# State-space heads and attention heads of a two-block mixer in one interleaved order, with the spreading products on all 128 rows

## What is computed

```python
def ssd_chunked(x, dt, A, Bm, Cm):
    a_cum = jnp.cumsum(a, axis=-1)
    seg = jnp.exp(jnp.where(causal, a_cum[..., :, None] - a_cum[..., None, :], -jnp.inf))
    cb = jnp.einsum('bclhn,bcshn->bhcls', Cm, Bm)
    y_diag = jnp.einsum('bhcls,bcshp->bclhp', cb * seg, xdt)      # 8 state-space heads of 64
...
def fox_mixer(q, k, v, f_raw, f_b):                                # 4 attention heads with a forget gate
    c = jnp.cumsum(log_f, axis=1).transpose(0, 2, 1)
    s = jnp.einsum('bqhd,bkhd->bhqk', q[:, q0:q1], k[:, :q1]).astype(jnp.float32) * scale
    return s + (c[:, :, q0:q1, None] - c[:, :, None, :q1])
...
def mla_mixer(...):                                                # 4 attention heads
        s = jnp.einsum('bqhd,bkhd->bhqk', q_nope[:, q0:q1], k_nope[:, :q1])
        s = s + jnp.einsum('bqhr,bkr->bhqk', q_rope[:, q0:q1], k_rope[:, :q1])
...
    mix = jnp.concatenate([y_ssd, y_fox.astype(h.dtype), y_mla.astype(h.dtype)], axis=-1) @ w_out[l]
```

## Time and profile before

| | before |
|---|---|
| median of 3 runs | 2350.14 us |
| the profiled execution | 2333.99 us |
| its span | 2331.9 us |
| TensorE busy | 2142.1 us (92%) |
| VectorE busy | 1222.7 us (52%) |
| ScalarE busy | 875.1 us (38%) |
| GpSimd busy | 709.2 us (30%) |
| mean granted clock of TensorE | 0.942 |

### The profile page before, as it was taken

One profiled execution on the slowest core, in us unless ns is written; L12 is line 12 of the kernel. 1 busy time (PEld: TensorE's weight loads), 2 busy tenths in 40 slices (PEclk: granted clock), 3 DMA queues, 4 the chain that ended last, 5 costly groups with the idle time before them and its releaser, 6 DMA issues.

```text
span 2331.9 us, 40609 instructions
## 1 busy us (share of the span) xinstructions
PE 2142.1 (92%) x17634; PEld 1918.1 (82%) x17634; DVE 1222.7 (52%) x2199; ACT 875.1 (38%) x1262; POOL 709.2 (30%) x316
## 2 busy tenths in 40 slices
PE   4989988999889989999999898899999998889997
PEld 3867866889887868898999785699989997758897
DVE  6155445763672447653652665565265419437652
ACT  0442111444443223544433444243343335334443
POOL 0340001314672003126315550131551175204124
PEclk9998997999998989999999997899999998869999
DMA  8563441455343003554454340244444543203552
GB/s 327 229 258 146 147 161 61 155 187 185 141 157 115 2 2 128 193 185 163 163 181 165 128 160 1 91 164 180 170 142 177 179 165 116 102 16 139 189 185 87
DMA packets 49681, 340.43 MB, mean 146 GB/s; under 512 B 6368, under 2 KB 8416, under 8 KB 8672
## 3 DMA queue, kind: packets, MB, share of 16 engines
q1 hardware_dynamic: 49504, 337.84, 40.2%
HBM read 336.77 MB, written 1.05 MB: 145 GB/s over the span
## 4 chain that ended last, share of the span: by engine, by line
PE 82%; DVE 11%; ACT 2%; issue 2%; DMA 2%; POOL 1%; SPq 0%; ACTq 0%; DVEq 0%; POOLq 0%
PE bank L529 81%; DMA ada_ring<-ada 2%; POOL ring_low L2442 1%; PE bank L535 1%; DVE arena L1842 1%; DVE small L1837 1%; DVE arena L1827 1%; ACT high L1429 1%; DVE arena L1870 1%; DVE arena_parts L1865 1%; DVE ZZ L2049 0%; DVE arena L1857 0%; DVE ada_ring L2350 0%; DVE arena L2393 0%; DVE small L2300 0%
## 5 line engine op out<-in xcount | busy, mean ns | idle before, releaser
L529 PE MATMUL bank<-arena_parts,high 128*128 128x272 f32 (+2 forms) x4512 | 1023.9, 315 | 60.0 <-ACT arena_parts L1454 38.0
L529 PEld LDWEIGHTS bank<-arena_parts,high 128*128 128x128 f32 x4512 | 748.0, 191 | 110.0 <-issue 48.7
L529 PE MATMUL bank<-arena_parts,ring_low 128*128 128x272 f32 (+2 forms) x2736 | 781.0, 288 | 0.0
L1429 ACT ACTIVATE high<-ring 128x2048 fp32r<-128x2048 f32 x237 | 453.2, 1914 | 676.9 <-PE bank L529 591.4
L2442 POOL TENSOR_TENSOR ring_low<-ring,high 128x2048 fp32r<-128x2048 f32 x105 | 485.5, 4627 | 721.0 <-ACT high L1429 721.0
L529 PEld LDWEIGHTS bank<-arena_parts,ring_low 128*128 128x128 f32 (+1 forms) x2736 | 522.6, 191 | 1.0
L1878 DVE TENSOR_TENSOR ring_low<-ring,high 128x2048 fp32r<-128x2048 f32 x132 | 303.9, 2302 | 180.6 <-ACT high L1429 180.6
L529 PE MATMUL bank<-hidden_high,high 128*128 128x256 f32 (+1 forms) x1056 | 303.2, 287 | 0.0
L529 PE MATMUL bank<-hidden_low,high 128*128 128x256 f32 (+1 forms) x1056 | 301.1, 285 | 0.0
L529 PE MATMUL bank<-hidden_high,ring_low 128*128 128x256 f32 (+1 forms) x1056 | 300.2, 284 | 0.0
L2442 POOL TENSOR_TENSOR hidden_low<-arena,hidden_high 128x256 fp32r<-128x256 f32 (+1 forms) x132 | 111.9, 850 | 575.1 <-DVE hidden_high L1894 575.1
(11 more groups left out here) (317 smaller groups left out, 2291.8 us busy)
## 6 DMA issues: line engine op xcount, KB each, us to landing
ring<-stream SPq DMA_DIRECT2D x269, 1024.0 KB, 4.8
ada_ring<-ada SPq DMA_DIRECT2D x48, 1024.0 KB, 6.0
con<-consts SPq DMA_DIRECT2D x1, 1542.5 KB, 11.3
con<-consts SPq DMA_DIRECT2D x1, 1040.0 KB, 7.0
arena<-xin SPq DMA_DIRECT2D x1, 1024.0 KB, 11.5
out<-arena SPq DMA_DIRECT2D x2, 512.0 KB, 2.9
prob_even<-consts SPq DMA_DIRECT2D x1, 320.0 KB, 11.6
par<-params SPq DMA_DIRECT2D x1, 272.5 KB, 9.3
```

The lines of the kernel that those rows point to most:

```text
L529: ins = nc.tensor.matmul(o, l, r, start=start, stop=stop_, skip_group_check=True)
L1429: act(high[:, q % HIGHS], ring[:, s % RING], ACT.Copy).then_inc(a.sig(high_ready), 1)
```

## The change

**Rows.** The running sums and the forget-gate products take all 128 rows of `sel12` and of `arena[:, 9, 5]` and `arena[:, 9, 6]` instead of 12. The added rows of `sel12` are zeros already; for the added rows of the tiles, VectorE clears `arena[:, 9, 5:7]` at the start of `mixer(l)`.

**Order.** TensorE does running sums 0 to 3, logits 0, running sums 4 and 5, state-space product 0, running sums 6 and 7, state-space product 1, logits 1, state-space products 2 and 3, and then the transposes. VectorE and ScalarE follow in an order that fits. The norm's sums by `ones` move behind logits 2, its root behind the last exponentials, and its reciprocal to the end of VectorE's part.

**Memory and semaphores.** The running sums use banks 6, 7, 4 and 5 instead of 0 to 3, so that logits 0 has banks 0 to 3. `prob(2)` and `prob(3)` move from slot 6 to the memory behind `EE`. ScalarE's decay exponentials get a semaphore of their own, and `sloped` counts every head.

```diff
         def prob(h):
-            return (prob_even, arena[:, 2, 4:7], arena[:, 6, 0:3], arena[:, 6, 3:6])[h % 4]
+            o = 8 * 432 + 3 * TALL * (h % 2)
+            return (prob_even, arena[:, 2, 4:7])[h % 4] if h % 4 < 2 else spare[:, o:o + 3 * TALL].rearrange("p (i t) -> p i t", i=3)
...
-                for h in range(8):
-                    b = h % 4
+                def running_sum(h):
+
+                    b = (6, 7, 4, 5, 4, 5, 4, 5)[h]
                     if h < 4:
                         eng.wait_ge(*freed(b))
-                    elif h % 2 == 0:
-                        eng.wait_ge(sloped, pe.nth(sloped))
-                    mm(bank[b][:, 0:T], cm("sel12", P, P * h, 12), arena[0:12, 9, 5, 0:T], True, True,
+                    else:
+                        eng.wait_ge(sloped, pe.nth(sloped, 3 if h == 4 else 1))
+                    mm(bank[b][:, 0:T], cm("sel12", P, P * h), arena[:, 9, 5, 0:T], True, True,
                        hold=True).then_inc(told(b, "vector"), 1)
...
-                                m = mm(to(e), cm("sel12", qn, P * (8 + h), 12), arena[0:12, 9, 6, 0:kn], False, True, hold=i)
+                                m = mm(to(e), cm("sel12", qn, P * (8 + h)), arena[:, 9, 6, 0:kn], False, True, hold=i)
...
+                for h in range(4):
+                    running_sum(h)
+                for b in range(4):
+                    eng.wait_ge(*freed(b))
                 logits(0)
...
+                running_sum(4)
+                running_sum(5)
+                state_space(0)
+                running_sum(6)
+                running_sum(7)
+                state_space(1)
+                eng.wait_ge(logits_masked, pe.nth(logits_masked, 6))
+                logits(1)
+                state_space(2)
+                state_space(3)
+                eng.wait_ge(sloped, pe.nth(sloped, 2))
                 for p in range(4):
-                    if p == 0:
-                        eng.wait_ge(logits_masked, pe.nth(logits_masked, 6))
-                        logits(1)
                     for e in range(2):
                         turned(2 * p + e)
                     if p < 2:
                         eng.wait_ge(logits_masked, pe.nth(logits_masked, 6))
                         logits(p + 2)
+                    if p == 0:
+                        eng.wait_ge(a2p, pe.nth(a2p))
+                        for g in range(2):
...
                     attended(p)
```

ScalarE, whose whole new order of this part is:

```diff
+                decays(0)
+                decays(1)
                 exps(0)
                 exps(1)
...
+                decays(2)
+                decays(3)
+                exps(2)
+                exps(3)
+                eng.wait_ge(v2a, a.nth(v2a))
+                act(arena[:, 2, 0:4, 0:T], arena[:, US, 0:4, 0:T], ACT.Square).then_inc(a.sig(a2p), 1)
+                turned(0)
+                turned(1)
+                turned(2)
+                exps(4)
+                turned(3)
+                exps(5)
+                attended(0)
+                turned(4)
+                exps(6)
+                turned(5)
+                exps(7)
+                eng.wait_ge(v2a, a.nth(v2a))
+                act(small[:, 0:2, 0:T], small[:, 0:2, 0:T], ACT.Sqrt).then_inc(a.sig(a2v), 1)
+                attended(1)
+                turned(6)
+                turned(7)
                 attended(2)
                 attended(3)
```

VectorE:

```diff
             def mixer(l):
                 eng.wait_ge(*v.last)
+                nv.memset(arena[:, 9, 5:7, :], 0.0).then_inc(v.sig(vstep), 1)
+                eng.wait_ge(*v.last)
...
+                slopes(0)
+                slopes(1)
+                weighted(0)
                 masked(0)
                 masked(1)
+                slopes(2)
+                weighted(1)
+                ssd_out(l, 0)
+                slopes(3)
+                weighted(2)
+                ssd_out(l, 1)
+                masked(2)
+                weighted(3)
+                masked(3)
+                ssd_out(l, 2)
+                ssd_out(l, 3)
+                finish(0)
+                finish(1)
                 for g in range(2):
                     eng.wait_ge(full_for_vector[6 + g], v.nth(full_for_vector[6 + g]))
                     nv.tensor_scalar(small[:, g, 0:T], bank[6 + g][:, 0:T], 1.0 / 256, EPS_LN, ALU.mult, ALU.add).then_inc(v.sig(free["vector"][6 + g]), 1)
...
+                nv.memset(cols[:, 59:60], 0.0).then_inc(v.sig(v2a), 1)
+                for h in range(2, 6):
                     finish(h)
...
+                    masked(h + 2)
+                finish(6)
+                finish(7)
+                eng.wait_ge(a2v, v.nth(a2v))
+                nv.reciprocal(small[:, 0:2, 0:T], small[:, 0:2, 0:T]).then_inc(v.sig(vstep), 1)
```

More of the change, by code:

```diff
@@ L1380, in mixer @@
                         logits(p + 2)
+                    if p == 0:
+                        eng.wait_ge(a2p, pe.nth(a2p))
+                        for g in range(2):
+                            eng.wait_ge(*freed(6 + g))
+                            for k in range(2):
+                                m = mm(bank[6 + g][:, 0:T], cm("ones"), tl(2, 2 * g + k, T), k == 0, k == 1, hold=k)
+                                if k:
+                                    m.then_inc(closing(6 + g, "vector"), 1)
                     attended(p)
@@ L1713, in mixer, with decays @@
                     act(MV[0:sn, i], bank[b][0:sn, 256:512], ACT.Copy).then_inc(a.sig(free["scalar"][b]), 1)
[L1714 to L1718 removed]
+                def decays(j):
+                    eng.wait_ge(sloped, a.nth(sloped, 2))
+                    act(EE[:, 2 * j:2 * j + 2], EE[:, 2 * j:2 * j + 2], ACT.Exp).then_inc(a.sig(decays_ready), 1)
                 def exps(h):
@@ L1737, in attended @@
                     act(tl(US, 4 + p, T), bank[b][:, 0:T], ACT.Copy).then_inc(a.sig(free["scalar"][b]), 1)
+                decays(0)
+                decays(1)
                 exps(0)
                 exps(1)
-                for h in range(8):
-                    if h < 6:
-                        exps(h + 2)
-                    turned(h)
-                    if h == 3:
-                        eng.wait_ge(v2a, a.nth(v2a))
-                        act(small[:, 0:2, 0:T], small[:, 0:2, 0:T], ACT.Sqrt).then_inc(a.sig(a2v), 1)
-                    if h in (3, 5):
-                        attended(h // 2 - 1)
+                decays(2)
[20 more added lines that the diff above has]
+                turned(7)
                 attended(2)
@@ L2350, in slopes @@
                             nv.tensor_scalar(EE[0:sn, h, PK[i]:PK[i] + T - s0], bank[b][0:sn, s0:T], decay_col(i, h, sn), 0.0,
[L2351 removed]
+                                             ALU.add, ALU.min).then_inc(v.sig(sloped if i == 2 else vstep), 1)
                 def weighted(j):
[L2355 removed]
+                    eng.wait_ge(decays_ready, v.nth(decays_ready))
                     x = EE[:, 2 * j:2 * j + 2]
                     nv.tensor_tensor(x, x, CB[:, j // 2].unsqueeze(1).to_broadcast([P, 2, 432]), ALU.mult).then_inc(v.sig(decayed), 1)
[L2359 to L2372 removed]
                 def masked(h):
@@ L2399, in mixer @@
                     nv.tensor_scalar(small[:, g, 0:T], bank[6 + g][:, 0:T], 1.0 / 256, EPS_LN, ALU.mult, ALU.add).then_inc(v.sig(free["vector"][6 + g]), 1)
-                for h in range(8):
-                    if h < 6:
-                        masked(h + 2)
-                    if h == 3:
-                        nv.memset(cols[:, 59:60], 0.0).then_inc(v.sig(v2a), 1)
-                    finish(h)
-                    if h == 5:
-                        eng.wait_ge(a2v, v.nth(a2v))
-                        nv.reciprocal(small[:, 0:2, 0:T], small[:, 0:2, 0:T]).then_inc(v.sig(vstep), 1)
+                nv.memset(cols[:, 59:60], 0.0).then_inc(v.sig(v2a), 1)
+                for h in range(2, 6):
+                    finish(h)
+                    masked(h + 2)
[3 more added lines that the diff above has]
+                nv.reciprocal(small[:, 0:2, 0:T], small[:, 0:2, 0:T]).then_inc(v.sig(vstep), 1)
                 eng.wait_ge(*v.last)
```

41 lines of the change are left out of this document (7 added, 34 removed).

## The result

| | before | changed |
|---|---|---|
| median | 2350.04 us, 4 runs (2349.17 to 2351.91) | 2317.72 us, 4 runs (2317.15 to 2322.09) |
| the profiled execution | 2333.99 us | 2317.15 us |
| its span | 2331.9 us | 2315.1 us |
| mean granted clock | 0.942 | 0.949 |
| first running sum to output projection, first and second layer | 65.1 and 65.8 us | 56.0 and 56.1 us |

The two profiled executions are 16.8 us apart. The gap between 32.3 and 16.8 us is what most of the following is about.

The account below looks back on a forecast made before the run. No engine was taken as full: engines wait in a chain, with TensorE at a low clock. 9.2 less 0.6 us a layer, 17.2 in both, rounded to 16.5, from 2350.1 gave 2333.6 us; 8-in-10 range 2324 to 2345.

Parts of the forecast that it names:

- The chain through the new order: Mixer, first layer: gain followed to the first transposes (11.0 us), those of head 2 (10.0) and the end (9.2).
- VectorE's wait for the norm's sums: Sign in the changed profile's mixer: VectorE idle some 7 us before its scaling of the norm's sums.
- The memset: VectorE's clearing of two tiles ahead of the mixer's convolution: 0.6 us lost in each layer, bounds 0 and 1.2.
- a wait for the SiLU 0.6 us longer: Sign at the mixer's start: TensorE waits 0.6 us longer for the SiLU that follows the convolution.
- small waits: Waits between engines left out of the mixer chain: the gain of 17.2 us was rounded down to 16.5 for them.
- the base: Last step, whole kernel: the gain of 16.5 us was taken from the median of 2350.1, giving 2333.6 us.
- The range: Whole kernel: 2324 to 2345 us, to hold 8 in 10, reaching to the full-clock and the rows-do-nothing rivals.
- Rival B: Mixer: wide rows do nothing for the clock; the order alone gains 3.6 us a layer, 2344.1 us; chance 0.18.
- Rival C: Mixer: clock falls at the first wait and stays low, 5.8 us lost a layer, 2361.7 us; chance 0.05.
- Rival A: Mixer: full clock throughout the stretch, 2325.7 us; chance 0.14.
- Rival D: Mixer: the extra wait for the norm's sums and VectorE's tail eat the gain, about 2350 us; chance 0.03.
- The rule of the Trainium skill: Mixer's forget-gate products: 128 rows can't hide beside 64-row ones, losing part of 0.27 us per instruction; taken as nothing.

Follow-up runs that it names:

- experiment 1: The kernel before, run again with no edit: median 2344.41 us over 12 executions; its profiled execution took 2349.6 us, with mixer stretches of 61.3 and 65.0 us.
- experiment 4: The changed kernel, run again with no edit: median 2328.41 us over 12 executions, ratio 0.9949 against the kernel before.
- experiment 2: The changed kernel with 12-row products and no memset, so the new order alone: 2355.37 us, ratio 1.0045 against the kernel before.
- experiment 3: The kernel before, in its old order, with 128-row products and the memset: 2334.15 us, ratio 0.9975 against the kernel before.
- experiment 6: The changed kernel with the delta net's three spreads on 128 rows instead of 8: 2305.91 us, ratio 0.9860 against the kernel before.
- experiments 6 and 8: The second of these put the delta net's three spreads on 128 rows in the kernel before, mixer untouched: 2324.63 us, ratio 0.9953.

## Why the prediction was right and wrong

**The chain through the new order was right.** The first transposes were put at 21.8 us and came at 20.3; those of head 2 at 33.4, and came at 32.8; the end at 55.9, and it came at 56.03 and 56.13. Of the gain of 9.2 a layer 9.05 and 9.67 are there, against the profile from which it was forecast (5.3 and 8.9 against the stretches of experiment 1). The steps behind it hold as well: logits 0 and 1 at full clock, the low level after the wait for finish 0, the tail of root, reciprocal and scaling, line 2447 as the releaser of the output projection. VectorE's wait for the norm's sums was put at about 7 us and is 9.36. The reason is logits 2, which I priced at 5.5 us and which ran 7.33 us, nearly all at the low level. Logits 3, put at 6.0, took 7.36. The sum held all the same, because the first transposes came 1.5 us early and ran in 0.77 and 0.90 us where I had put 1.25: the clock fell 1 us behind the wait and not at it.

**The memset** was put at 0.6 us and moves what follows by 0.74 in the first layer. The sign that went with it, a wait for the SiLU 0.6 us longer, didn't come (4.0 and 2.4 us as before), and in the second layer its time can't be seen: the stretch between the mixers, which has it, is 0.44 us shorter.

**The sum against the profiled execution was right**: 16.5 forecast, 16.8 measured, 2317.5 against 2317.15. That it is right within 0.3 us is luck: the 0.7 us taken off for small waits stand where the up-projections lost 1.4 at a clock that has nothing to do with the change, and the old mixer alone differs by 3.8 us between two executions.

**The step that failed is the last one, the base.** It reads: the median, "which stands 16.2 above that execution", less the same 16.5, is 2333.6. That takes the 16.2 us between a profiled execution and a median as a constant belonging to both kernels. It is none. The kernel before has executions from 2329 to 2357 us, which differ in TensorE's clock, most of all in the delta-net layer (131.3 us in one profile, 146.6 in the other). All four runs of its median took 2349 to 2352 us, as those of the long kind do, and the profiled one is of the short. The four of the changed kernel lie within 5 us of its profiled one, which is of the short kind as well. So the median moved by the 16.8 us between the profiled executions and by 16.05 - 0.57 = 15.5 more, since before's median stands 16.05 above its profiled execution and the changed kernel's 0.57: together 32.3. With more executions on both sides the change is worth less than the result says: experiment 4 has 10.6 us between the medians, and the means (2341.2 over 83 and 2327.2 over 12) are 14.0 apart. The range failed in the same step: it held the bounds of the mixer's clock and nothing for the spread of the executions, of which the table's 16.2 us was the sign. A forecast of 2317.5, made from the profiled execution, with some 15 us to either side for that spread would have held the measured median.

**The reason was right in kind and wrong in its shares.** I took the order as the gain and the rows as what lets it come. Rival B, wide rows that do nothing, was priced at 2344.1 us with 3.6 us a layer gained by the order alone. Experiment 2 is that case, the new order without wide rows, and it loses 3.0 and 0.4 us. The rows alone are worth 6.3 and 6.9 (experiment 3), both together 9.05 and 9.67. So the order isn't a gain of its own; it is worth 2.8 and 2.7 us on top of the rows, and without them it is longer than all three profiles of the old order. Why it then stays at the low clock for 37 us wasn't found. The sums by `ones`, behind which the clock was up in the old order, aren't what lifts it in the new one: in experiment 2 and in the changed kernel (from 1435.6 us on) it is up again within logits 2, ahead of them. Rival C put the point from which it costs at a mean clock of 0.65, and experiment 2, at 0.62 and 0.63, stands just behind that point.

**Rows count for the clock here, and busy time alone doesn't explain it.** Experiment 2 and the changed kernel have the same instructions in the same order, but for the memset. Both start the stretch without a gap, and only the one with 12 rows falls, at 3.5 us. Over the stretch it is the busier, 58.93 of 68.07 us against 46.19 of 56.03, and has the lower clock, 0.62 against 0.81; the second layers agree (0.63 against 0.82). The Trainium skill, "TensorE: Matmul & The Clock Gate", Part 1, tells of the gate by how busy the engine was; this pair of runs doesn't agree with that alone, and experiment 6 says the same with 32 instructions behind one wait. Rows alone don't explain it either: 24 state-space instructions of 128 rows ran 3.85 us without a gap at 0.50 in experiment 2 (1434.13 to 1437.98 us), and in experiment 1 the clock fell behind 9 us in which TensorE was busy for 8.95. Rival A, full clock throughout, fell with logits 2 and 3 at 0.53 and 0.52 and with the tail at 0.50. Rival D fell with the stretches.

**No hiding between row groups.** The forget-gate products cost nothing more with 128 rows than with 12: at full clock, four of them at the end of logits 1 take 1.09 us against 1.08. The rule of the Trainium skill, "TensorE: Matmul & The Clock Gate", Part 3, weighed in the prediction, costs nothing in this kernel.

**What stays open.** Why the first runs of the kernel before stood together in the long kind and those of the changed kernel in the short one: the later sessions show both kinds of both. With 18 of 83 later executions at 2349 us or more, four independent ones would all stand there about once in 450 times, so something that those four shared is likely, and it wasn't found. In the middle of the delta net, in the recurrence of its state over the chunks, the clock falls in some executions and in others not, behind the same instructions; what decides it was not found. The fall in the middle was read from profiles and not made on purpose by an experiment; only the part behind the spreading products was (experiments 6 and 8). What makes the part ahead of the delta net differ by up to 8.3 us between profiles wasn't looked into.

## What to carry to other kernels

A product with 12 rows of contraction cost the same time here as one of 128 and, where such products stood close together, TensorE stayed at half clock. So try padding them with zeros where the clearing is cheap, and do it before any reordering: here the new order gained nothing without it. Ahead of any forecast, look how far the profiled execution stands from the median: a gap of 0.7%, 16.2 us here, says that executions differ by as much as this change gains, and it belongs into the range and not into the base. For such a kernel compare executions of the same kind stage by stage, or many on both sides.

## What the runs showed of the hardware

- Gapless or nearly gapless work with many narrow products didn't bring the clock up: 14.02 us of 8-row products without a gap, at 0.50, and 37.4 us at 94% busy and 0.50 in experiment 2, with 12-row and 64-row products and some of 128 rows between them. The first 32 instructions with 128 rows came up to full clock on the way and took 8.86 us (experiment 6).
- Rows cost no time by themselves: eight instructions of 272 columns took 2.10 us with 12 rows and with 128 (profiles of before and after).
- Executions of one and the same program differed by 28 us in 2340 (83 executions), with a correlation of -0.94 between span and mean clock. Of 15.7 us between two profiled ones, 15.3 lay in one layer (131.3 and 146.6 us), with the same instructions and the same busy time of the other engines there; smaller differences of either sign lay elsewhere.
- The clock also fell where TensorE had been busy for 8.95 of the last 9 us and waited for only 0.38 us, among 64-row and 128-row products of 64 and 128 columns: eight of 64 rows then took 1.80 us instead of 1.00 (experiment 1).
